# Mixture-of-experts output written block by block: plain first scatter, gather at the last expert, norm and store inside the expert loop

## What is computed

```python
weights = p_group * jax.nn.softmax(top_val, axis=-1)
expert_idx = (g_sel[:, None] * EXPERTS_PER_GROUP + top_idx)        # two different experts for each token
...
def run_block(args):                                               # 128 rows of one expert
    toks, e = args
    xb = h_pad[toks]
    return (jax.nn.silu(xb @ w_gate[e]) * (xb @ w_up[e])) @ w_down[e]
ys = ys.reshape(n_slots, -1) * slot_w[:, None]
out = jnp.zeros((T + 1, ys.shape[1])).at[slot_tok].add(ys)[:T]     # a token's two results are summed
...
x = x + hier_moe(h2, ...)
y = rms_norm(x, final_norm_g)                                      # y_prompt (4096 rows), y_sample (128 rows)
```

## Time and profile before

| | us |
|---|---|
| median of 3 runs | 3280.58 (3279.65 to 3287.41) |
| the profiled execution | 3276.18, its span 3274.4 |
| first stage, about | 0 to 2204 |
| stages meet | 2204 to 2243 |
| expert stage | 2243 to 3162 |
| closing stage | 3162 to 3274 |

### The profile page before, as it was taken

The page is one execution under the profiler, slowest core; times in us unless marked ns, Lnnn a source line. Parts: engine busy times, 40 slices in busy tenths (PEclk is TensorE's granted clock), DMA queues, the critical chain, the costliest instruction groups (busy, mean ns, idle before and its releaser), DMA issues. The chain is left out here.

```text
span 3274.4 us, 35981 instructions
## 1 busy us (share of the span) xinstructions
PE 3098.6 (95%) x10721; PEld 1679.5 (51%) x10721; DVE 1364.4 (42%) x4111; ACT 832.0 (25%) x1505; POOL 691.9 (21%) x1594
## 2 busy tenths in 40 slices
PE   7999999999999999999999999976999999999960
PEld 3555555555555555555555555553444444444430
DVE  4544654555455546545554555452111111111114
ACT  2222332232232323222322232221111111111123
POOL 1122122212211221122122111101222222222226
PEclk9999999999999999999999999978999999999985
DMA  7010100100010101011110100119876767678559
GB/s 254 27 33 27 45 27 32 40 31 32 26 45 26 32 26 45 26 32 39 32 32 26 45 26 20 48 43 304 228 206 186 189 172 212 175 215 225 141 149 343
DMA packets 148899, 316.00 MB, mean 97 GB/s; under 512 B 13948, under 2 KB 86201, under 8 KB 148748
## 3 DMA queue, kind: packets, MB, share of 16 engines
q1 hardware_dynamic: 123116, 228.64, 20.8%
q0 software_dynamic: 25632, 85.67, 11.4%
HBM read 215.50 MB, written 98.78 MB: 96 GB/s over the span
## 5 line engine op out<-in xcount | busy, mean ns | idle before, releaser
L364 PE MATMUL PB<-arena,hT 128*128 128x512 f32 x2640 | 1165.1, 594 | 3.2 <-DVE arena L968 3.2
L364 PEld LDWEIGHTS PB<-arena,hT 128*128 128x128 f32 x2640 | 495.4, 191 | 578.7 <-issue 574.8
L1376 PE MATMUL PB<-arena,hT 128*128 x1296 | 569.3, 592 | 1.0 <-DVE hT L1460 1.0
L473 PE MATMUL PB<-arena,tT 128*128 128x512 f32 x1056 | 461.5, 595 | 0.7 <-ACT tT L649 0.7
L1376 PEld LDWEIGHTS PB<-arena,hT 128*128 128x128 f32 x1296 | 246.2, 190 | 310.7 <-issue 310.7
L993 POOL TENSOR_TENSOR spare<-neg_half 128x1 f32<-128x1 f32 x545 | 118.7, 218 | 1081.0 <-ACT hT L663 615.9
L473 PEld LDWEIGHTS PB<-arena,tT 128*128 128x128 f32 x1056 | 198.1, 190 | 237.7 <-issue 236.8
L1415 PE MATMUL SS<-arena,xdt 128*128 x640 | 287.9, 592 | 0.0
L1466 DVE TENSOR_TENSOR gv<-ycat,PB 128x256 f32<-128x256 f32 x81 | 34.1, 422 | 569.8 <-ACT ycat L1439 569.8
L830 DVE TENSOR_TENSOR x_res<-x_res,PB 128x512 f32<-128x512 f32 x66 | 45.3, 687 | 397.7 <-PE PB L473 397.7
L755 DVE SCALAR_TENSOR_TENSOR xc<-xT,cols,xc 128x128 f32<-128x128 f32 x768 | 210.0, 346 | 2.3
(11 more groups left out here) (291 smaller groups left out, 3593.0 us busy)
## 6 DMA issues: line engine op xcount, KB each, us to landing
arena<-in_w_gate SPq DMA_DIRECT2D x32, 1024.0 KB, 7.1
arena<-in_w_up SPq DMA_DIRECT2D x32, 1024.0 KB, 9.5
arena<-in_w_down SPq DMA_DIRECT2D x32, 1024.0 KB, 5.1
x_rows<-x_res SPq DMA_DIRECT2D x34, 512.0 KB, 2.7
h_rows<-h SPq DMA_DIRECT2D x34, 512.0 KB, 3.5
arena<-x_rows SPq DMA_DIRECT2D x33, 512.0 KB, 5.4
out<-arena SPq DMA_DIRECT2D x33, 512.0 KB, 4.2
x_in<-in_x_prompt SPq DMA_DIRECT2D x32, 512.0 KB, 3.9
```

The source lines that it names most:

```text
L364: mm = nc.tensor.matmul(out, hT[u][:, k, :], w_in_sb[:, k, col:col + n], start=k == 0, stop=k == KD - 1)
L473: mm = nc.tensor.matmul(PB[b][:, :], tT[:, k, :], w_out_sb[:, k, b * 512:(b + 1) * 512], start=k == 0, stop=k == KD - 1)
L1376: mm = nc.tensor.matmul(PB[u][:, :], hT[u][:, k, :], arena[:, bass.ds(slot + k * 2 * DE, 2 * DE)], start=k == 0, stop=k == KD - 1)
```

## The change

A token has two experts, and blocks are worked off in order of experts, so one of the two results always comes first. In `dve_slots` the token number in the list of the later one gets 8192 added (`LATER`). From the lists three index tables follow: `tok_i` (all rows, for the gather of h2), `first_i` (a row number out of bounds where this block is not the token's first), `last_i` (out of bounds where it is not the last), `smp_i` (the same for the sample rows). Rows out of bounds are skipped by the DMA. A step of block b now is:

- the weighted result y is scattered plainly to `first_d` by `first_i`;
- x2 rows and the earlier results are gathered by `last_i` (`residual`, `earlier`), each one block ahead, the earlier results only when the scatter of the block before has landed;
- VectorE adds y + x2, then the earlier result, into `f`; ScalarE squares and sums; GpSimd makes mean and power; VectorE scales; GpSimd scatters f to y_prompt and y_sample. Rows for which this block isn't the last one are computed and not stored.

In the first stage each tile also stores 128 rows into `first_d` (so that it is never unset), the pad tile of x2 is no longer stored, and two small VectorE operations are added. The list gather goes to another buffer and no longer waits for the stores of h2. The closing stage is gone.

```diff
-DVE_TURN, POOL_TURN = 100, 32
+LATER = 8192
+DVE_TURN, POOL_TURN = 104, 32
 GB = 4
...
-        x2_d = nc.dram_tensor("x2_rows", [T + P, D], F32).ap()
+        x2_d = nc.dram_tensor("x2_rows", [T, D], F32).ap()
         h2_d = nc.dram_tensor("h2_rows", [T + P, D], F32).ap()
+        first_d = nc.dram_tensor("first_rows", [T, D], F32).ap()
...
+        f_buf = [take(D) for _ in range(2)]
+        m_buf = [take(D), xbc[:, :]]
+        xr_buf = [flat_of(xT[:, :, :])[:, 0:D], g2_b[:, :]]
...
-            for k, weight in enumerate((w1, w2)):
-                st.inc(V.tensor_copy(slots_f[:, 2 + 2 * k:3 + 2 * k], tok_id[:, :]))
+            for k, (mine, other, weight) in enumerate(((k1, k2, w1), (k2, k1, w2))):
+                st.inc(V.tensor_scalar(slots_f[:, 2 + 2 * k:3 + 2 * k], mine, other, float(LATER), ALU.is_gt, ALU.mult))
                 st.inc(V.tensor_copy(slots_f[:, 3 + 2 * k:4 + 2 * k], weight))
+            st.wait()
+            for k in range(2):
+                st.inc(V.tensor_tensor(slots_f[:, 2 + 2 * k:3 + 2 * k], slots_f[:, 2 + 2 * k:3 + 2 * k], tok_id[:, :], ALU.add))
             st.wait()
...
+                sp.dma_start(at_tile(first_tiles, i - 1), g2_b[:, :]).then_inc(first_set, 16)
             if tn.end:
-                sp.dma_start(at_tile(x2_tiles, NT), x_res[v][:, :]).then_inc(x2_stored, 16)
...
-            V.tensor_copy(tok_i[:, :], PB[1][:, 0:P]).then_inc(s["lists_out"], 1)
+            st.link(V.tensor_copy(first_i, PB[1][:, 0:P]))
+            V.tensor_scalar(tok_i[:, :], first_i, LATER - 1, None, ALU.bitwise_and).then_inc(s["lists_out"], 1)
...
+            early, last_f = lnb_b[:, 0:P], lnb_b[:, P:2 * P]
+            st.link(V.tensor_copy(last_f, first_i))
+            st.link(V.tensor_scalar(early, last_f, float(LATER), 2.0 * LATER, ALU.is_lt, ALU.mult))
+            st.link(V.scalar_tensor_tensor(out=last_f, in0=last_f, scalar=float(-LATER), in1=early, op0=ALU.add, op1=ALU.add))
+            st.inc(V.tensor_copy(last_i, last_f))
+            st.link(V.tensor_scalar(early, last_f, float(SEQ), 2.0 * LATER, ALU.is_lt, ALU.mult))
+            st.link(V.scalar_tensor_tensor(out=last_f, in0=last_f, scalar=float(-SEQ), in1=early, op0=ALU.add, op1=ALU.add))
+            V.tensor_copy(smp_i, last_f).then_inc(s["idx_out"], 1)
...
             pool.wait_ge(scattered, 32 * NT)
-            pool.wait_ge(h2_stored, 16 * (NT + 1))
             nc.gpsimd.indirect_dma_start(out=list_rows, out_offset=None, in_=slot_d.rearrange("(r n) a -> r (n a)", n=P),
                                          in_offset=bass.IndirectOffsetOnAxis(ap=row_i[:, 0:1], axis=0)).then_inc(lists_loaded, 16)
             pool.wait_ge(s["lists_out"], 2)
             pool.wait_ge(s["tables"], 1)
+            pool.wait_ge(h2_stored, 16 * (NT + 1))
+            def rows_of(dram, out, index, b, done, last=T - 1):
+                nc.gpsimd.indirect_dma_start(out=out, out_offset=None, in_=dram, bounds_check=last, oob_is_err=False,
+                                             in_offset=bass.IndirectOffsetOnAxis(ap=index[:, b:b + 1], axis=0)).then_inc(done, 16)
+            def rows_to(dram, src, index, b, done, last=T - 1):
+                nc.gpsimd.indirect_dma_start(out=dram, in_=src, in_offset=None, bounds_check=last, oob_is_err=False,
+                                             out_offset=bass.IndirectOffsetOnAxis(ap=index[:, b:b + 1], axis=0)).then_inc(done, 16)
             def gather(b):
                 n = b % GB
                 after(pool, s["gx_T"], 2 * (b - GB + 1))
-                nc.gpsimd.indirect_dma_start(out=g_buf[n], out_offset=None, in_=h2_d[:, :],
-                                             in_offset=bass.IndirectOffsetOnAxis(ap=tok_i[:, b:b + 1], axis=0)).then_inc(gathered[n], 16)
+                rows_of(h2_d[:, :], g_buf[n], tok_i, b, gathered[n], T + P - 1)
+            def residual(b):
+                after(pool, s["x2_added"], b - 1)
+                rows_of(x2_d[:, :], xr_buf[b % 2], last_i, b, x2_back[b % 2])
+            def earlier(b):
+                after(pool, first_kept, 16 * b)
+                after(pool, s["fin_sq"], b - 1)
+                rows_of(first_d[:, :], m_buf[b % 2], last_i, b, first_back[b % 2])
             def step(b):
-                gather(b + 3)
-                after(pool, added, 16 * b)
                 for k in range(2):
                     pool.wait_ge(s[f"dn_out{k}"], b + 1)
-                nc.gpsimd.indirect_dma_start(out=x2_d[:, :], in_=y_buf[b % GB], in_offset=None, compute_op=ALU.add,
-                                             out_offset=bass.IndirectOffsetOnAxis(ap=tok_i[:, b:b + 1], axis=0)).then_inc(added, 16)
+                rows_to(first_d[:, :], y_buf[b % GB], first_i, b, first_kept)
+                gather(b + 3)
+                residual(b + 1)
+                pool.wait_ge(s["fin_sq"], b + 1)
+                r = rs[:, b % 2:b % 2 + 1]
+                nc.gpsimd.tensor_scalar(r, sq[:, b % 2:b % 2 + 1], 1.0 / D, EPS, ALU.mult, ALU.add).then_inc(s["fin_mean"], 1)
+                pool.wait_ge(s["fin_mean"], b + 1)
+                nc.gpsimd.tensor_tensor(r, r, neg_half[:, 0:1], ALU.pow).then_inc(s["fin_r"], 1)
+                earlier(b + 1)
+                pool.wait_ge(s["fin_out"], b + 1)
+                rows_to(y_prompt.rearrange("a n d -> (a n) d"), f_buf[b % 2], last_i, b, y_stored[b % 2], SEQ - 1)
+                rows_to(y_sample.rearrange("a n d -> (a n) d"), f_buf[b % 2], smp_i, b, y_stored[b % 2], P - 1)
                 if b % 2 and b // 2 >= SURE - 1:
                     pool.wait_ge(gathered[(b + 3) % GB], 16 * ((b + 3) // GB + 1))
+                    pool.wait_ge(x2_back[0], 16 * ((b + 1) // 2 + 1))
+                    pool.wait_ge(first_back[0], 16 * ((b + 1) // 2))
             for n in range(3):
                 gather(n)
-            return over_pairs(pool, step)
+            pool.wait_ge(s["idx_out"], 1)
+            pool.wait_ge(x2_stored, 16 * NT)
+            pool.wait_ge(convs_stored, 16 * CW)
+            pool.wait_ge(first_set, 16 * NT)
+            residual(0)
+            used = over_pairs(pool, step)
+            for u in range(2):
+                pool.wait_ge(y_stored[u], 32 * used)
+            nc.gpsimd.tensor_tensor(spare[:, 3:4], neg_half[:, 0:1], neg_half[:, 0:1], ALU.mult).then_inc(s["all_stored"], 1)
...
-                after(act, added, 16 * (b - GB + 1))
+                after(act, first_kept, 16 * (b - GB + 1))
+                after(act, s["x2_added"], b - GB + 1)
                 nc.scalar.activation(y_buf[b % GB][:, 0:512], SS[:, 0, :], ACT.Copy, scale=wt[:, b:b + 1]).then_inc(s["dn_out0"], 1)
+                act.wait_ge(s["first_added"], b + 1)
+                nc.scalar.activation(h2[:, :], f_buf[b % 2], ACT.Square, accum_out=sq[:, b % 2:b % 2 + 1]).then_inc(s["fin_sq"], 1)
...
-                after(dve, added, 16 * (b - GB + 1))
+                after(dve, first_kept, 16 * (b - GB + 1))
                 V.tensor_scalar(y_buf[b % GB][:, 512:], SS[:, 1, :], wt[:, b:b + 1], None, ALU.mult).then_inc(s["dn_out1"], 1)
-            dve.wait_ge(x2_stored, 16 * (NT + 1))
+                f = f_buf[b % 2]
+                for k in range(2):
+                    dve.wait_ge(s[f"dn_out{k}"], b + 1)
+                dve.wait_ge(x2_back[b % 2], 16 * (b // 2 + 1))
+                after(dve, y_stored[b % 2], 32 * (b // 2))
+                V.tensor_tensor(f, y_buf[b % GB], xr_buf[b % 2], ALU.add).then_inc(s["x2_added"], 1)
+                dve.wait_ge(s["x2_added"], b + 1)
+                after(dve, first_back[b % 2], 16 * ((b + 1) // 2))
+                V.tensor_tensor(f, f, m_buf[b % 2], ALU.add).then_inc(s["first_added"], 1)
+                dve.wait_ge(s["fin_r"], b + 1)
+                V.scalar_tensor_tensor(out=f, in0=f, scalar=rs[:, b % 2:b % 2 + 1], in1=gf_b, op0=ALU.mult,
+                                       op1=ALU.mult).then_inc(s["fin_out"], 1)
...
-        def sp_phase3(sp):
-            used = pairs_used(sp)
-            sp.wait_ge(added, 32 * used)
-            whole(sp, used)
-            for r in range(FB):
-                load_row(sp, 0, r)
-            def turn(q, r):
-                t = FB * q + r
...
```

More of the change, by code:

```diff
@@ L302, in build @@
         assert sample_end <= SLOT_AT[0], sample_end
-        FB = 4
-        x_row = [take(D) for _ in range(FB)]
         used[0] = WSLOTS * WSLOT
         gf_b = take(D)
-        fin_o = [take(D) for _ in range(2)]
-        fin_s = take(D)
+        f_buf = [take(D) for _ in range(2)]
+        m_buf = [take(D), xbc[:, :]]
+        xr_buf = [flat_of(xT[:, :, :])[:, 0:D], g2_b[:, :]]
         def half(b):
@@ L1479, in dve_phase2 @@
             gate(0)
-            return over_pairs(dve, step)
-        LAST = NP // FB
-        def over_out(eng, turn):
-            for r in range(FB):
-                turn(0, r)
-            with eng.Fori(1, LAST - 1) as q:
-                for r in range(FB):
-                    turn(q, r)
-            for t in range(NP - FB, NT):
```

(28 more changed lines are left out.)

66 lines of the change are left out of this document (19 added, 47 removed).

## The result

The kernel after takes 3303.2 us (median, 3292.9 to 3313.2) against 3280.9 us (3279.7 to 3287.4) for the kernel before, measured beside each other: a ratio of 1.0056, 95% interval 1.0036 to 1.0076. It is slower by 0.56%, where 3246 us and faster was forecast; the time lies inside the range of 3183 to 3350.

A forecast was written before the change was run, and what follows sets the result against it. It took TensorE to bound the expert stage and the closing stage to be pure serial time. 3276 - 99 + 56 + 6 + 2 = 3241, plus 4.4 from profiled execution to median: 3246 us, range 3183 to 3350.

The forecast's parts named there:

- The closing stage: End of the kernel: 112 us of serial time go, one block's finish of some 13 us remains; 99 us saved.
- The stall: Expert stage, before the row transposes: TensorE waits 0.7 us a block for the gather, 56 us, plus 6 for first blocks.
- The start: Gather's issue on GpSimd: at 2.7 us, since VectorE's first add holds the scatter until 1.4, done at 2.35.
- The landing: Gather's rows arrive 3.9 us after its start, at 6.6, 0.5 late for TensorE's transposes at 6.1.
- The weight loads: Gather beside weight loads: one block in twelve pays 2.5 us, 0.2 on average; first blocks, 6 us in all.
- GpSimd's queue: GpSimd in the expert stage: six indirect DMAs a block take 11.5 us against a period of 12.1; covered by 0.6.
- VectorE and ScalarE: Expert stage: three and one more operations a block, 5 and 1.2 us, in engines busy 20%; cost nothing.
- Where the stages meet: Between first and expert stage: half a megabyte more to load and two short VectorE links add 2 us.
- (a): Rival, expert stage: adds don't hold the scatter, gather lands at 5.5, no stall; 3187 us; 28%.
- (b): Rival, row transposes: gather issued at 4.0, lands near 8.1, TensorE waits 2.0 a block; 3350 us, slower; 20%.
- (c): Rival, expert stage: GpSimd becomes the bound; 3494 us with 1.59 an issue, 3310 with 1.2; 7%.
- (d): Rival, expert stage: idle gaps bring TensorE's clock down to half; over 3400 us; 3%.

The follow-up runs named there:

- the kernel with small loads: Kernel after, with the weight loads of the fifth and all later experts cut to an eighth of their size: 3265.5 us, ratio 0.9935.
- the kernel four ahead with small loads: Kernel after, gathering for block b+4 instead of b+3, with weight loads of the fifth and later experts cut to an eighth: 3189.3 us, ratio 0.971.
- the variants that stall 2.8 a block: Kernel before, gather issued behind the accumulating scatter: 3546.7 us; kernel after, gather issued one place later, behind the residual's gather: 3453.6 us.
- its repeat: Kernel after, nothing changed, measured again beside the others on the same chip: 3301.8 us, ratio 1.0063.
- the run without the adds: Kernel after without VectorE's two adds; ScalarE copies the block's output into the buffer that is normed: 3292.4 us, ratio 1.0027.

## Why the prediction was wrong, step by step

*The closing stage* (forecast -99, measured -95.5): right within 3.5 us. Up to the landing of the last scatter the sum holds: the fetch for the next block took 2.03 instead of 0.97, held by the scaling beside it, but mean and power took 0.8 instead of 1.25 and the last scatter's issue ends at 10.6, not 11.2; GpSimd stops waiting 13.2 behind the last output, at 3298.9, where 13 was forecast. What the sum lacked stands behind that, the end of the program: a last GpSimd instruction of 3.1 us, which ran beside the last store in the kernel before.

```profile
L110 POOLq DRAIN  x1: 3105/3105/3105, 3298.9 to 3298.9; - x1
```

*The stall* is the term that failed, in size, and with it the sign. Forecast 0.7 x 80 plus 6, 62 us; measured 112. Its pieces:
- The start: forecast 2.7, measured 2.47. The mechanism is right: the scatter is held until the add's end. The add ends at 1.32 (forecast 1.4), the scatter's issue 0.85 behind it (forecast 0.95), at 2.17, and in all 79 blocks the scatter beside this add ends 0.84 to 0.89 behind it. A little too dear (-0.2 a block).
- The landing: "I take 3.9", measured 4.4 without any weight load. This is the first mis-sized step, +0.5 a block, 40 us. I built it from SP's plain load and store (3.6 and 2.7 in the earlier trace rows) with GpSimd's issue put in; the nearest row was the gather itself, at 5.6 to 6.1, and I treated that as an upper bound to be far undercut. The scatter ahead explained 0.1 of it in quiet blocks. The other end of my range for a stall, a landing of 4.6, was much nearer the truth than the value that I took.
- The weight loads: forecast "one block in twelve" at 2.5, and 6 for the first blocks, 22 us together; measured 40 (0.51 x 79). I read the slowest of the old landings and guessed at its frequency. In the kernel after, weights moved during the gather in 43 of 79 blocks, and delayed it by 0.5 in the mean of 40 of them and by 2 in three.
- Blocks in which GpSimd was late, 0.1 a block, weren't in the forecast (see the last section).
Together 0.74 + 0.51 + 0.1 = 1.35, and 1.41 with the 0.06 behind each wait, of the measured 1.42. The two intervals at half the clock, 0.04, lie within the 0.51: the kernel with small loads had none.

*GpSimd's queue* (forecast: covered): right for the kernel after, which idles 2.5 a block, and shown by the kernel four ahead with small loads, whose periods are all 11.4. The bounds check and the skipped rows neither shortened nor lengthened an issue: 1.0.

*VectorE and ScalarE* (forecast nothing): right for the kernel after, since the stall itself gave them room. The wait on the earlier result that I had named as what would spoil the number appeared once the stall was gone, 0.24 a block under weight loads.

*Where the stages meet* (+2, measured +3.5): the first gather came 1.2 later behind the index arithmetic, which the forecast had hidden, and the first 32 gate/up matmuls took 2.0 longer because the clock was at half until 44 us after the last x2 store instead of 37.5. *First stage* (0): right.

*The rivals.* (a), no stall, is out. (b) had the place and the sign: the gather much too late, deciding from 1.14 a block. Its reason was wrong (a start at 4.0 by a hold on both adds: the gather comes up when the second add has 0.1 left); a start at 2.47 with landings of 4.0 to 7.4 (4.8 in the median) passed the same point: the rows were there at 7.3 in the median block, against its 7.2. Its price of 2.0 was too high, which is why the loss is only 0.56%. (c) and (d) are out for this kernel; (d) is seen in the variants that stall 2.8 a block.

The chances were wrong where a sum of two ends 6.6 was compared with a need of 6.1 and a break-even of 7.2: 0.6 us of landing decided the sign, and the landing was a choice between 3.3 and 6.1. That deserved even odds, not 68 to 26.

## What to carry to other kernels

Before work is added to an in-order queue, list for each prefetch in it the lead that it has now and the lead that it will have, and compare with the slowest landing in the trace, not with the median; buy the lead with depth (a block further ahead) and not with a place in the queue. An issue moved ahead of a wait in the code gains less than it seems if the queue is behind by then (here 0.95 of 1.42 us a block), and a wait for a landing in that queue delays all that stands behind it. And price a transfer by the row of the same kind, on the same queue, before any other.

## What the runs showed that I had not expected

- *Skipped rows shorten the landing, not the issue.* Each bounds-checked transfer is issued in 1.0, however many rows it skips. How many it moves goes from none to all of 128 by the block, so a median hides what they do. The residual's fetch in the kernel with four ahead and small loads, in three blocks in which it moves 90 rows or more, and in three in which it moves fewer than 10 (us from issue to landing, min/median/max):

```profile
DMA to landing us min/median/max: 5.2/5.2/5.3
```

```profile
DMA to landing us min/median/max: 3.3/3.4/3.5
```

  In the same stretches the earlier result's fetch lands in 5.4 to 6.8 and in 3.1. A skipped row shows as a packet of 4 bytes: in the expert stage there are 41104 on GpSimd's queue against 2528 before, where nothing is skipped and each of 158 transfers has 16.
- *An issue is held until the end of the add or the scaling beside it.* In the kernel after, 144 of the 146 issues that begin during an add end 0.84 to 0.94 behind the add's end, and all 78 that begin during the scaling 0.93 to 0.95 behind its end; the other two began with the add and took 1.0. Beside VectorE's 128x512 operations on TensorE's output an issue takes what it takes alone, 0.99 to 1.03 in 55 cases. So what the hold costs is what is left of the operation: 0.34 for the scatter, which begins 0.46 ahead of the add's end, and 1.0 for the earlier result's fetch, which begins 1.09 ahead of the scaling's (kernel after, duration in ns, min/median/max):

```profile
L1352 POOL DMA_INDIRECT xbc<-first_rows,lng_b x40: 1060/2027/2045, 2279.6 to 3279.8; - x40
```

  The Trainium skill, "SBUF — State Buffer", Who interferes with whom, infers that a two-input tensor_tensor leaves descriptor generation alone; these runs show it held until the add's end, so the measurement decides against it. "DMA: Bandwidth & Descriptors", Anatomy of one DMA, of the Trainium skill, gives an estimate of 3.2 us for these rows; measured 4.4.
- *GpSimd pauses.* In six blocks of the kernel after, the last five of them fifteen apart, the gather started 1.2 to 1.3 late, at 3.65 to 3.8, with nothing in the profile that it waited for. The kernel after with small loads has one such pause here:

```profile
2495.55 1.18 POOL L1357 DMA_INDIRECT first_rows<-tT,lng_b  x1 [2.81 <-DVE tT L1529]
2498.34 1.04 POOL L1352 DMA_INDIRECT x_in<-h_rows,tok_i  x1 [1.61 <-issue]
```

- *The clock and the stall.* With a mean stall of 1.2 to 1.3 us in 12.8 there were 2, 3 and 5 intervals of 3.4 us at half the clock in the expert stage (after, its repeat, and the run without the adds); with 2.8 in 14.8 there were 24 and 26 (85 and 92 us). A longer stall costs more than itself.
